# Expert joins: the residual add in halves, unscaled rows transposed, scale and shift in the copies and on GpSimd

## The reference

```python
for i in range(2):
    h = diff_attention(x, ...) if i == 0 else rwkv7_time_mix(x, ...)   # both end in a product with a 1024x1024 w_o
    x = layer_norm(ALPHA * x + h, ln1_g[i], ln1_b[i])                  # the change is about this line
    f = hier_moe(x, rg_w[i], rg_b[i], re_w[i], re_b[i], w_gu[i], w_down[i])
    x = layer_norm(ALPHA * x + f, ln2_g[i], ln2_b[i])

def layer_norm(x, g, b):
    mu = mean(x); var = mean((x - mu) ** 2)
    return (x - mu) * rsqrt(var + 1e-5) * g + b
```

## Time and profile before

| | |
|---|---|
| median of 3 runs | 2008.54 us (2007.52 to 2009.27) |
| the profiled execution | 2007.26 us, of which 2005.5 us is the span from the first to the last instruction |
| busy share of the span | PE 83%, DVE 30%, ACT 18%, POOL 1% |
| mean granted TensorE clock | 0.928 of full |
| read from HBM | 533.71 MB, of which the experts' weights in two stages at some 427 GB/s |
| layer 0: join to the first expert | about 761 to 791 us |
| layer 1: join to the first expert | about 1515 to 1544 us |

### The profile page before, as it was taken

How to read it: one execution, slowest core, us unless ns; L and a number is a source line. 1 busy time by engine, 2 the same in 40 slices (tenths; PEclk the granted TensorE clock), 3 DMA queues, 4 the chain that set the end, 5 groups by cost and what they waited for, 6 DMA issues and landing times.

```text
span 2005.5 us, 28819 instructions
## 1 busy us (share of the span) xinstructions
PE 1673.0 (83%) x12498; PEld 1039.1 (52%) x12498; DVE 595.8 (30%) x1041; ACT 367.9 (18%) x727; POOL 28.2 (1%) x19
## 2 busy tenths in 40 slices
PE   9999999999999997766666897899987768666665
PEld 6898885888885855221221332767855223221211
DVE  1234221243321255211111123573365212211103
ACT  1443101343211251000000001242211000000001
POOL 0000000000000000000000000000300000000000
PEclk9999999999999997988888899899997988987977
DMA  9341444252355436999999997221154999999994
GB/s 374 105 160 73 159 176 162 81 147 85 147 191 207 168 149 255 427 427 426 426 428 427 427 417 315 106 85 66 67 231 184 427 427 425 426 427 427 427 426 200
DMA packets 48221, 537.01 MB, mean 268 GB/s; under 512 B 4532, under 2 KB 12980, under 8 KB 15032
## 3 DMA queue, kind: packets, MB, share of 16 engines
q1 hardware_dynamic: 46752, 528.27, 64.4%
q10 hardware_dynamic: 1304, 6.51, 0.8%
HBM read 533.71 MB, written 1.05 MB: 267 GB/s over the span
## 4 chain that ended last, share of the span: by engine, by line
PE 61%; DMA 32%; DVE 4%; ACT 1%; issue 1%; DVEq 0%; POOL 0%; ACTq 0%; POOLq 0%
PE ps L430 51%; DMA arena<-in_moe_w_gu 27%; PE ps L442 7%; DMA ring<-in_moe_w_gu 5%; PE ps L448 3%; DVE x L1476 1%; DVE arena L1465 1%; ACT arena L2312 0%; DVE arena L1476 0%; PE ps L437 0%; DVE small L1499 0%; ACT arena L2308 0%; DVE hT L1488 0%; DVE hb L1465 0%; DVE arena L1480 0%
## 5 line engine op out<-in xcount | busy, mean ns | idle before, releaser
L430 PE MATMUL ps<-hT,ring 128*128 128x256 f32 (+1 forms) x1792 | 371.1, 369 | 0.0
L430 PEld LDWEIGHTS ps<-hT,ring 128*128 128x128 f32 (+1 forms) x1792 | 318.2, 186 | 44.7 <-issue 1.8
L442 PE MATMUL ps<-arena 128*32 128x512 f32 (+1 forms) x1348 | 205.6, 692 | 88.4 <-DMA arena<-in_moe_w_gu 70.1
L2312 ACT ACTIVATE arena<-ps 128x512 f32<-128x512 f32 (+4 forms) x146 | 93.8, 643 | 864.1 <-PE ps L442 503.5
L442 PE MATMUL ps<-ring,arena 128*32 128x512 f32 x1248 | 175.4, 692 | 92.1 <-DMA ring<-in_moe_w_gu 71.7
L1465 DVE TENSOR_TENSOR arena<-arena,ps 128x256 f32<-128x256 f32 (+2 forms) x78 | 41.1, 527 | 526.4 <-ACT arena L2308 443.4
L430 PE MATMUL ps<-arena 64*64 64x64 f32 (+8 forms) x2080 | 161.0, 295 | 28.7 <-ACT arena L2601 22.3
L442 PEld LDWEIGHTS ps<-arena 128*32 128x32 f32 (+1 forms) x1348 | 49.1, 125 | 225.4 <-DMA arena<-in_moe_w_gu 102.0
L430 PEld LDWEIGHTS ps<-arena 64*64 64x64 f32 (+3 forms) x2080 | 109.4, 154 | 79.1 <-ACT arena L2601 48.9
L442 PEld LDWEIGHTS ps<-ring,arena 128*32 128x32 f32 x1248 | 37.8, 118 | 206.3 <-DMA ring<-in_moe_w_gu 102.7
L430 PE MATMUL ps<-ring,hT 128*128 128x256 f32 (+3 forms) x512 | 140.6, 433 | 0.9 <-DVE hT L1488 0.9
(11 more groups left out here) (188 smaller groups left out, 1294.6 us busy)
## 6 DMA issues: line engine op xcount, KB each, us to landing
arena<-in_moe_w_gu SPq DMA_DIRECT2D x57, 2048.0 KB, 41.3
ring<-in_moe_w_gu SPq DMA_DIRECT2D x49, 2048.0 KB, 41.3
ring<-in_moe_w_down SPq DMA_DIRECT2D x35, 2048.0 KB, 41.6
arena<-in_moe_w_down SPq DMA_DIRECT2D x29, 2048.0 KB, 41.3
extra<-in_moe_w_gu SPq DMA_DIRECT2D x22, 2048.0 KB, 41.3
ring<-in_w_merge SPq DMA_DIRECT2D x16, 2048.0 KB, 8.5
ring<-in_w_in SPq DMA_DIRECT2D x9, 2048.0 KB, 7.3
ring<-in_attn_w_qkv SPq DMA_DIRECT2D x6, 2048.0 KB, 7.3
```

Source lines behind the costliest of these rows:

```text
L430: i = t.matmul(o, l, r, start=first, stop=last, skip_group_check=True)
L442: i = t.matmul(o, l, r, start=first, stop=last, skip_group_check=True)
L2312: s.activation(o, a, ACT.Copy).then_inc(*act.one(name))
```

## The change

Per join and tile:

- PE names the end of each half of the product (`a`, `b`), DVE adds and takes statistics of the left half when it is there, then of the right.
- DVE makes (x - mean) / root in two halves of one pass each, without scale and shift rows. PE transposes a half when it is there, naming `a` and `b`.
- The copies of the transposed blocks apply scale and shift: they are columns now (`ln1g`, `ln1b`, new in the column table `vec`), so each 128x128 block is an instruction of its own with two column operands: four on ACT (Identity with scale and bias), four on DVE. PE multiplies the left blocks with the routing columns behind ACT's copies, the right behind DVE's.
- `x` itself gets scale and shift on POOL, two passes of 128x1024 for each tile, behind the tile's transposes and behind POOL's memset. PE's first gather waits for both tiles, DVE waits for the second before it writes gate tables over `m.lnr`.

```diff
@@ -750,15 +750,19 @@
 
         name = f"{n} out{i}"
         if ks[0] == 0 and halves[0] == 0:
-            tile(name, (dve, f"{n} ln{i}"))
+            tile(name, (dve, f"{n} x{i}"))
             ps.held.add(ps.of[name])
             for half in range(2):
                 t.wait_ge(*m.w.landed(f"{n} wo{half}"))
         p = ps(name)
         for done in ready:
             t.wait_ge(*done)
-        mm([(p[:, 512 * half:512 * half + 512], srcT[:, k, i * P:(i + 1) * P], wcols(m.w(f"{n} wo{half}"), KT, 512)[:, k, :],
-             k == 0, k == KT - 1) for half in halves for k in ks], name if ks[-1] == KT - 1 and halves[-1] == 1 else None)
+        for half in halves:
+            done = ks[-1] == KT - 1
+            mm([(p[:, 512 * half:512 * half + 512], srcT[:, k, i * P:(i + 1) * P], wcols(m.w(f"{n} wo{half}"), KT, 512)[:, k, :],
+                 k == 0, k == KT - 1) for k in ks], name + "ab"[half] if done else None)
+            if done and half:
+                pe.name(name)
 
     def join(n, l, tiles):
         pe.name(f"{n} end")
...
@@ -766,13 +770,15 @@
             ps.held.discard(ps.of[f"{n} out{i}"])
             name = f"{n} xT{i}"
             p = tile(name, (act, name + " out a"), (dve, name + " out b"))
-            t.wait_ge(*dve(f"{n} ln{i}"))
-            tr([(p[:, k * P:(k + 1) * P], x[:, i, k * P:(k + 1) * P], idn) for k in range(KT)], name)
+            for half in range(2):
+                t.wait_ge(*dve(f"{n} normed{i}{half}"))
+                tr([(p[:, k * P:(k + 1) * P], x[:, i, k * P:(k + 1) * P], idn) for k in range(4 * half, 4 * half + 4)], name + "ab"[half])
 
             p = tile(f"moe{l} route{i}", (dve, f"moe{l} logits{i}"))
-            t.wait_ge(*act(name + " out a"))
-            t.wait_ge(*dve(name + " out b"))
-            mm([(p[:, 0:36], hT[:, k, i * P:(i + 1) * P], m.rw36[:, 36 * (KT * l + k):36 * (KT * l + k + 1)], k == 0, k == KT - 1) for k in range(KT)], f"moe{l} route{i}")
+            for half in range(2):
+                t.wait_ge(*(dve(name + " out b") if half else act(name + " out a")))
+                mm([(p[:, 0:36], hT[:, k, i * P:(i + 1) * P], m.rw36[:, 36 * (KT * l + k):36 * (KT * l + k + 1)], k == 0, k == KT - 1)
+                    for k in range(4 * half, 4 * half + 4)], f"moe{l} route{i}" if half else None)
 
     def diff_attention():
         d = m.diff
...
@@ -1125,6 +1131,8 @@
                         t.br(N + "over").branch_hint(back)
 
         t.wait_ge(*dve(M + "0 oh"))
+        for i in range(NT):
+            t.wait_ge(*pool(f"{('da', 'rw')[l]} ln{i}"))
         for half in range(2):
             gather(psum[0][:, 512 * half:512 * half + 512], half, M + f"first gather{half}")
         t.wait_ge(*dve(M + "0 places"))
...
@@ -1767,24 +1775,28 @@
         v.wait_ge(*pe(n))
         cp(m.hT[:, 4:8, i * P:(i + 1) * P], ps(n)[:, 512:1024].rearrange("p (k s) -> p k s", k=4), n + " out b")
 
-    def layer_norm(n, src, rows, tiles, name):
-
-        for i in tiles:
-            stt(x[:, i, :], x[:, i, :], ALPHA, src(i), MUL, ADD, f"{n} x{i}")
-            mv = spread(f"{n}{i}", x[:, i, :], f"{n} var{i}")
-            v.wait_ge(*act(f"{n} std{i}"))
-            rec(mv[:, 1:2], mv[:, 1:2])
-            v.wait_ge(m.rows_landed, 16 * (rows + 1))
-            stt(x[:, i, :], x[:, i, :], mv[:, 0:1], m.lnr[:, 0, :], SUB, MUL)
-            stt(x[:, i, :], x[:, i, :], mv[:, 1:2], m.lnr[:, 1, :], MUL, ADD, name(i))
-
-    def join(n, l, rows, tiles):
+    def join(n, l, tiles):
         dve.name(f"{n} end")
         for i in tiles:
-            v.wait_ge(*pe(f"{n} out{i}"))
-            layer_norm(f"{n}{i}", lambda _: ps(f"{n} out{i}"), rows, (i,), lambda i: f"{n} ln{i}")
-            v.wait_ge(*pe(f"{n} xT{i}"))
-            cp(m.hT[:, 4:8, i * P:(i + 1) * P], ps(f"{n} xT{i}")[:, 512:1024].rearrange("p (k s) -> p k s", k=4), f"{n} xT{i} out b")
+            st, mv, p = sml(f"{n}{i}{i} st", 12), sml(f"{n}{i}{i} mv", 2), ps(f"{n} out{i}")
+            for half in range(2):
+                c = slice(512 * half, 512 * half + 512)
+                v.wait_ge(*pe(f"{n} out{i}" + "ab"[half]))
+                stt(x[:, i, c], x[:, i, c], ALPHA, p[:, c], MUL, ADD, f"{n} x{i}" if half else None)
+                after_own()
+                v.bn_stats(st[:, 6 * half:6 * half + 6], x[:, i, c]).then_inc(*dve.one())
+            after_own()
+            v.bn_aggr(mv, st).then_inc(*dve.one())
+            ts(mv[:, 1:2], mv[:, 1:2], 1e-5, None, ADD, None, f"{n}{i} var{i}")
+            v.wait_ge(*act(f"{n}{i} std{i}"))
+            rec(mv[:, 1:2], mv[:, 1:2])
+            for half in range(2):
+                c = slice(512 * half, 512 * half + 512)
+                ts(x[:, i, c], x[:, i, c], mv[:, 0:1], mv[:, 1:2], SUB, MUL, f"{n} normed{i}{half}")
+            v.wait_ge(*pe(f"{n} xT{i}b"))
+            for k in range(4, KT):
+                ts(m.hT[:, k, i * P:(i + 1) * P], ps(f"{n} xT{i}")[:, k * P:(k + 1) * P], vcol("ln1g", 8 * l + k), vcol("ln1b", 8 * l + k),
+                   MUL, ADD, f"{n} xT{i} out b" if k == KT - 1 else None)
         for i in tiles:
             route(l, i)
 
...
@@ -1937,6 +1949,7 @@
                 if four == 0:
                     dve.name(M + "0 oh")
                     behind_oh()
+                    v.wait_ge(*pool(f"{('da', 'rw')[l]} ln{0 if l == 0 else 1}"))
                 for q in range(2):
                     og5 = e.og[q].rearrange("p (t h e n) -> p t h e n", t=NT, h=2, e=2)
                     e2 = slice(4 * four + 2 * q, 4 * four + 2 * q + 2)
...
@@ -2480,11 +2493,14 @@
             s.wait_ge(*dve(f"{n} var{i}"))
             fn(mv[:, 1:2], mv[:, 1:2], ACT.Sqrt, f"{n} std{i}")
 
-    def join(n, tiles):
+    def join(n, l, tiles):
         act.name(f"{n} end")
         for i in tiles:
             layer_norm(f"{n}{i}", (i,))
-            tile_out(f"{n} xT{i}", m.hT, i)
+            s.wait_ge(*pe(f"{n} xT{i}a"))
+            for k in range(4):
+                fn(m.hT[:, k, i * P:(i + 1) * P], ps(f"{n} xT{i}")[:, k * P:(k + 1) * P], ACT.Identity,
+                   f"{n} xT{i} out a" if k == 3 else None, bias=vcol("ln1b", 8 * l + k), scale=vcol("ln1g", 8 * l + k))
 
     def rows(i):
 
...
@@ -2827,6 +2843,13 @@
         g.wait_ge(*act(n + " end"))
         g.wait_ge(*dve(n + " end"))
         g.memset(m.moe.acc, 0.0).then_inc(*pool.one(M + "acc zero"))
+        g.wait_ge(m.rows_landed, 16 * (2 if l == 0 else 4))
+        for i in ((1, 0), (0, 1))[l]:
+            xi = m.x[:, i, :]
+            g.wait_ge(*pe(f"{n} xT{i}b"))
+            for row, op, name in ((0, MUL, None), (1, ADD, f"{n} ln{i}")):
+                g.wait_ge(*pool.all())
+                g.tensor_tensor(xi, xi, m.lnr[:, row, :], op).then_inc(*pool.one(name))
         if l == 0:
             for i in range(NT):
 
...
@@ -3028,7 +3051,7 @@
 
 
 _VECS = (("norm_g", 16), ("qn", 4), ("kvn", 2), ("nb1", 4), ("nb2", 2), ("bm", 64), ("mu", 48), ("w0", 8), ("a0", 8),
-         ("kk", 8), ("ka", 8), ("rk", 8), ("subln", 1))
+         ("kk", 8), ("ka", 8), ("rk", 8), ("subln", 1), ("ln1g", 16), ("ln1b", 16))
 _ROWS = (("lam", 256), ("mb", 72), ("nb2v", 128))
 
 
...
@@ -3076,7 +3099,7 @@
         "nb2": colmaj(np.concatenate([i["nsa_b2"][:, 0], i["nsa_b2"][:, 0]], axis=1)), "bm": colmaj(i["b_merge"]),
         "mu": colmaj(i["rw_mu_2"]), "w0": colmaj(i["rw_w0_2"]), "a0": colmaj(i["rw_a0_2"]), "kk": colmaj(i["rw_k_k_2"]),
         "ka": colmaj(i["rw_k_a_2"]), "rk": colmaj(i["rw_r_k_2"]),
-        "subln": colmaj(i["attn_subln_g_2"]),
+        "subln": colmaj(i["attn_subln_g_2"]), "ln1g": colmaj(i["ln1_g_2"]), "ln1b": colmaj(i["ln1_b_2"]),
     }
     r = {
         "lam": i["attn_lambda_2"].reshape(-1),
```

More of the change, by code:

```diff
@@ L1868, in diff_attention @@
             oT_half(i, 1)
-        join("da", 0, 1, (1, 0))
+        join("da", 0, (1, 0))
     def route(l, i):
@@ L2280, in rwkv @@
             norm(1, half)
-        join("rw", 1, 3, range(NT))
+        join("rw", 1, range(NT))
     for l in range(L1):
@@ L2580, in diff_attention @@
         oT_half(0, 1)
-        join("da", (1, 0))
+        join("da", 0, (1, 0))
     def moe(l):
@@ L2793, in rwkv @@
             oT_half(i, half)
-        join("rw", range(NT))
+        join("rw", 1, range(NT))
     s.dma_start(x[:, 0], T["x"][0, 0:P]).then_inc(m.x_landed[0], 16)
```

## The result

| | before | changed |
|---|---|---|
| median, first comparison | 2008.15 us (8 runs) | 2016.25 us (8 runs), ratio 1.0036, 95% interval 1.0023 to 1.0049 |
| second | 2007.59 us | 2013.65 us (12 runs), 1.0027, 1.0016 to 1.0038 |
| third | 2007.65 us | 2012.25 us (11 runs), 1.0017, 1.0008 to 1.0026 |
| profiled execution, first | 2007.26 us (span 2005.5) | 2016.55 us (span 2014.8) |

The change costs time: 0.27% or 5.4 us as the mean of three comparisons. The forecast was 2014.0 us, 5.5 us above before, with a range from 2007.6 to 2015.5: the first median lies 0.75 us above that range, the two others inside it. How much of the 5.4 us the joins carry, and through which steps, is what follows.

What follows compares the result with a forecast made beforehand. The chain was PE for 61% and DMA for 32%, with DVE setting the joins' end. Per layer 0.27 plus 2.50 for POOL's interference, twice, gave +5.5 us: forecast 2014.0 us, range 2007.6 to 2015.5.

Steps and rivals of the forecast that it cites:

- one for one, and twice: Joins ahead of the expert stages: any change in their length reaches program time in full, in both layers.
- The add and statistics of the second tile in halves: DVE in the join: early left half wins nothing, split costs 2.93 us against 2.72, +0.21 a layer.
- DVE's copies: Transposed tiles: four 128x128 copies with two column scalars take 1.75 us for 0.69, +1.06 for each tile.
- The norm in one pass: DVE's second-tile row passes: one pass in halves lets PE's left transposes start earlier, -2.06 us a layer.
- The norm's +0.13 for standing behind POOL: Second tile's norm would start at 768.01 and stand until POOL's pass ends at 768.14, +0.13 us.
- The stall: DVE's routing: an SBUF scalar instruction stands until POOL's pass ends, 2.4 us a layer.
- Split route product: PE's routing product in halves of 1.8 us, over at 775.6 before DVE wants it at 776.4: covered.
- waits of PE and DVE on POOL: PE's gather and DVE's gate tables come over 6 us after POOL ends at 775.7: no cost.
- POOL undisturbing: POOL's passes disturb nobody; layers cost or win 0.5 us, 2009.1 us, 2007.5 to 2010.5; chance 0.30.
- The clock: TensorE's clock holds through a shorter PE pause, winning 2.4 us a layer; 2004.3 if POOL disturbs nobody; chance 0.09.
- The worse case: POOL's passes stretch too, or ACT table loads wait for data: 2.6 to 4.7 us more, about 2017.5; chance 0.04.
- the near row: Trace's DVE pass at 1434.21, one PSUM operand, 1.22 us beside POOL; by it alone the sum is +0.5 us.

Runs made afterwards that it cites:

- passes left out: Changed kernel without POOL's two passes over each tile and the waits on them, rows lacking scale and shift: 2009.43 us, ratio 1.0011.
- delay that was covered: Kernel before plus two idle DVE passes per join behind routing, ahead of the write of the places: 2008.62 us, ratio 1.0007.
- delay of 1.95 a layer: Kernel before plus two idle DVE passes per join ahead of routing: 2010.82 us against 2009.27, ratio 1.0006.
- second tensor in routing: Changed kernel with routing's one-tensor DVE instructions given a second SBUF input, a tensor of ones replacing a constant: 2012.61 us, ratio 1.0023.
- delay of 3.94 a layer: Kernel before plus four idle DVE passes per join ahead of routing: 2017.64 us, ratio 1.0043.
- both first, no passes: Changed kernel, both tiles added and normed before copies, without POOL's passes and their waits, rows lacking scale and shift: 2000.41 us, ratio 0.9950.
- both_first: Changed kernel reordered: DVE adds and norms both tiles before copying either, PE transposes both before route products, POOL's passes kept: 2012.53 us, ratio 1.0014.
- the last experiment: Changed kernel with scale and shift back on DVE, plain copies all on ACT, both tiles transposed before route products: 1999.87 us, 0.9952 to kernel before.

## Where the prediction was right and where not

**All joins and all medians.** A ratio times 2008 gives the added time; beside it stands what the joins of the same kernel's profile added to 58.95 us. All nine kernels, the changed one with its three comparisons:

| kernel | joins, us | program, us |
|---|---|---|
| passes left out | +0.24 | +2.2 |
| delay that was covered | +0.57 | +1.4 |
| both normed first | +1.16 | +2.8 |
| delay of 1.95 a layer | +3.53 | +1.2 |
| changed, three times | +3.99, +3.96, +3.92 | +7.2, +5.4, +3.4 |
| second tensor in routing | +4.09 | +4.6 |
| delay of 3.94 a layer | +7.95 | +8.6 |
| both first, no passes | -7.27 | -10.0 |
| copies on ACT | -10.04 | -9.6 |

Joins and program go together one for one, with a scatter of some 3 us that goes both ways; by its interval a program's figure is good to 2 or 3 us. So the prediction's "one for one, and twice" holds over a range of 18 us. The changed kernel's 7.2 us in the first comparison (interval 4.6 to 9.8) is more than its 4.0 us of joins; the other two intervals hold the 4.0. The mean of the three, 5.4, leaves 1.4 us that may be scatter or a small cost beside the joins: the runs don't decide it. In the profiles, one for each kernel, the scatter has a place: the mixer's stage took 259.30, 259.11 and 260.27 us in the changed kernel's profiles and 256.27 before, but also 255.80 with the second tensor in routing, whose joins are as long, 260.03 with the small delay, 256.80 with the large one and 262.79 with both tiles normed first and no passes, a kernel that is 10 us faster. It goes with the time at TensorE's 1.2 GHz that falls into it, summed from stretches of 1 us: 10.4 us before, 17.6 in the changed kernel's first profile, 18.0 in the one of 262.79. Why the stretches fall as they do I can't say; the length of the joins doesn't order them.

**The sum, term by term** (layer 0, in the order of the prediction):

- The add and statistics of the second tile in halves: 764.15 to 767.12 is 2.97 us for 2.72. Predicted 2.93. It stood behind the first tile's copies, as said, and `both_first` shows the other case.
- DVE's copies: 1.75 us twice, predicted 1.75; the second column scalar costs 0.06 like the first. ACT's four took 1.94, 0.46 each (2.2 allowed), with no table load of their own.
- The norm in one pass: 1.13 us for both halves, predicted 1.14; PE's left transposes start at 768.68, predicted 0.8 earlier than 769.49. Right.
- The norm's +0.13 for standing behind POOL: did not occur. It starts at 767.99, POOL's record ends at 768.19, and it runs its 1.13 as without POOL.
- Routing starts 0.24 us late; predicted +0.27, and +0.40 with that 0.13.
- The stall: 1.87 us (2.10 less 0.23), predicted 2.4. **This is the term that was mis-sized.** The mechanism is the one described, down to the scalar instruction that stands. Three things make the 0.53. A pass took 2.38, not 2.43, and the two were over 4.85 us after the last transpose (770.62), not 5.0: 0.15. DVE got 0.88 us done ahead of the stall where 0.7 were allowed, because its third instruction did not wait for the first pass to end: 0.18. And the hold ends earlier than POOL's record does: the stalled instruction ends at 775.49 and needs 0.23, so it began at 775.26, 0.21 before 775.47. The norm at 767.99 (0.20 before the record's end) says the same. Whether the pass itself ends earlier than its record, the profile can't tell.
- To the count +2.12, predicted +2.77; from DVE's first routing instruction to the count 9.64 us, for the 10.1 of the stall and the 7.8 of the first rival. To the first expert +2.19 and, in layer 1, +1.80. The gather was shorter: 5.18 for 6.21, as it began later against a rise of the clock that came at 788.1 in both profiles (it fell at 767.6 and was low for 20.5 us). In layer 0 this won nothing: DVE's gate tables, late by the whole 2.1, then held PE (0.57 us of idle ahead of the gates' transposes where there was none, 1.35 ahead of the expert where it was 1.04). In layer 1 nothing held PE behind the gather, and 0.33 of the 2.13 was won back.
- Sum of both: +3.99 instead of +5.5. The forecast of 2014.0 lies nearer to the medians than its sum to the joins; that is the scatter's doing and no merit of the sum.
- Split route product, waits of PE and DVE on POOL, larger column table: nothing, as said. POOL is done at 775.47, PE's gather starts at 785.26.

**The rivals.** POOL undisturbing: refuted by the 2.10 us and by the run without passes. The clock: refuted, the transposes at 768.68 take 1.94 us, with a granted clock of 0.50 from 768 to 771, the lower level; the shorter pause (2.80 us) changed nothing. What did change it, in layer 0, was coming earlier: in the last experiment the transposes are over when the clock falls. One profile is thin ground for that: the fall came at 764.8 in the changed kernel's second profile and at 767.6 in its first. The worse case: no table load waits for data (ACT's only one, at 771.81, is the one of the gates' Exp) and one instruction a layer stalls; two and three stalls came only where both tiles are normed first.

**The choice.** What had to be judged was whether the near row (a DVE pass with one operand in PSUM, unhurt at 1.22 us beside POOL) spoke for routing too. It didn't; with the operands in SBUF it is another case. The Trainium skill, SBUF — State Buffer, section "Who interferes with whom", says that a DVE instruction in a two-port mode, or with two SBUF inputs, blocks against a GpSimd instruction that reads SBUF, and that the first to issue keeps the pair until it ends. The runs agree, for the one-tensor kind with 2.10 and 2.06 us, for the one with two SBUF inputs with 2.12 and 2.00; in which mode the one-tensor instruction ran no run shows. It says too that `tensor_reduce` never contends on trn2: the 0.16 us reduction at 773.20, just ahead of the stall and beside POOL's pass, agrees.

## What to carry to other kernels

Work moved to an idle GpSimd isn't free when VectorE has small SBUF instructions on the path at that time: the smallest of them waited for the rest of POOL's pass, 2.1 us here for 0.23, and the price depended on where the passes fell. So look first at what DVE does in those microseconds: here reads from PSUM and reductions went through, the others from SBUF did not. Before splitting work in halves to start early, follow the later engine's program order: the half that is ready early wins nothing while a copy of the other tile stands ahead of it, while the other order and the early half together brought the start of routing forward by 3.8 us in layer 0 (11.07 to 7.23 behind the memset) and 3.6 in layer 1, without POOL's passes. Of that some 1.4 is the early half, an estimate from the add and the statistics of 0.69 each that leave the path. And where a join's change is some us of 2000, read the join in the profile and not the median: three comparisons of one kernel gave 3.4, 5.4 and 7.2 us for joins that agreed to 0.1.

## What the runs showed of the hardware

- A DVE instruction of 128x4 that works from SBUF to SBUF stood 1.87 to 1.90 us beside a POOL pass that reads two SBUF operands, with one tensor input or two alike (0.4 to 2.0 us with both tiles normed first, by what was left of the pass). At the seam between two passes one gets through (0.23 us at 772.94 in the changed kernel; with both tiles normed first, one tensor add of 0.19 us between two stalls), and the next stands until the next end. Reductions of 0.16 to 0.19 us ran beside the passes unhurt.
- DVE instructions that read PSUM and write SBUF ran at full speed beside the same passes: eight copies in 3.60 us, as without POOL.
- POOL's passes were not slowed much by DVE: 2.38 us beside routing, 2.43 in a row of four with the gaps between them, against 2.36. The hold on DVE ended about 0.2 us before the end of POOL's record: at the norm (0.20), at the changed kernel's stalls (0.21 and 0.19) and at the five stalls with both tiles normed first (0.19 to 0.28), each worked out as the stalled instruction's end less its undisturbed 0.23 or 0.25 us.
- On DVE 128x128 from PSUM takes 0.29 us as a copy, 0.35 with one column scalar and 0.41 with two. On ACT it is 0.46 us with two column operands and 0.367 with one.
